# Second block: each weight product in two halves of query rows, with attention steps set between the halves

## The reference

```python
proj = xn @ w_in[l]
sb_q, sb_k, sb_v, sw_q, sw_k, sw_v, sb_z, sw_z, g_sb, g_sw = jnp.split(proj, offsets, axis=-1)
o_sb = stick_breaking_attention(...)          # 8 heads of 64
q = rope(sw_q...); k = rope(sw_k...)
o_sw = sliding_window_sink_attention(...)     # 16 query heads, 2 key heads, window 128
y_sb = (o_sb * silu(sb_z)) @ w_branch_sb[l]
y_sw = (o_sw * silu(sw_z)) @ w_branch_swa[l]
merged = sigmoid(g_sb) * y_sb + sigmoid(g_sw) * y_sw
h = h + merged @ w_out[l]
return rms_norm_2(h, final_norm_gain)
```

## Time and profile before

| | |
|---|---|
| median of 3 runs | 1552.54 us (1546.03, 1552.54, 1552.65) |
| the profiled execution, its own time | 1551.99 us |
| its span, first to last instruction | 1550.2 us |
| mean granted TensorE clock over the span | 0.983 of 2.4 GHz |
| TensorE busy | 1504.0 us |
| VectorE busy | 1116.3 us |
| ScalarE busy | 904.5 us |

### The profile page before, as it was taken

The page is one execution under the profiler, slowest core; times in us unless marked ns, Lnnn a source line. Parts: engine busy times, 40 slices in busy tenths (PEclk is TensorE's granted clock), DMA queues, the critical chain, the costliest instruction groups (busy, mean ns, idle before and its releaser), DMA issues.

```text
span 1550.2 us, 19263 instructions
## 1 busy us (share of the span) xinstructions
PE 1504.0 (97%) x7580; PEld 1263.5 (82%) x7580; DVE 1116.3 (72%) x975; ACT 904.5 (58%) x770; POOL 134.9 (9%) x118
## 2 busy tenths in 40 slices
PE   6999999999989999999999999999999999999998
PEld 6869998897768888888888888888877687777786
DVE  6985455389778888888888988979789743343455
ACT  5564433355646777776777767676766553343443
POOL 3600000062010000000000000000172100000000
PEclk9999999999989999999999999999999998998999
DMA  9358964463379999999999999999999442322241
GB/s 329 133 176 282 327 233 166 136 197 115 126 274 354 353 394 363 378 378 355 396 355 371 392 347 406 348 375 380 368 407 336 151 164 82 109 84 80 82 163 55
DMA packets 118810, 407.67 MB, mean 263 GB/s; under 512 B 5824, under 2 KB 31600, under 8 KB 118752
## 3 DMA queue, kind: packets, MB, share of 16 engines
q1 hardware_dynamic: 114576, 392.84, 69.2%
q0 software_dynamic: 3104, 10.22, 1.8%
q10 hardware_dynamic: 1072, 3.80, 0.6%
HBM read 400.02 MB, written 18.87 MB: 270 GB/s over the span
## 4 chain that ended last, share of the span: by engine, by line
PE 83%; DVE 11%; issue 2%; ACT 2%; DMA 2%; ACTq 0%; DVEq 0%; SPq 0%
PE ps L465 22%; PE ps L466 22%; PE ps L467 22%; DVE low L449 3%; DVE yT L1909 3%; PE ps L2586 1%; DVE low L455 1%; PE ps L2259 1%; DMA raw<-in_moe_wg 1%; ACT high L444 1%; PE ps L1235 1%; DMA raw<-in_moe_wu 1%; PE ps L1256 1%; DVE xn L1846 1%; PE ps L1222 1%
## 5 line engine op out<-in xcount | busy, mean ns | idle before, releaser
L455 DVE TENSOR_TENSOR low<-raw,high 128x2816 fp32r<-128x2816 f32 (+1 forms) x168 | 522.1, 3124 | 99.7 <-ACT high L444 99.4
L444 ACT ACTIVATE high<-raw 128x2816 fp32r<-128x2816 f32 (+1 forms) x168 | 428.5, 2561 | 109.8 <-PE ps L467 53.6
L465 PE MATMUL ps<-high,xTm_hi 128*128 128x384 f32 (+2 forms) x1144 | 424.3, 371 | 13.3 <-DVE low L449 7.2
L466 PE MATMUL ps<-low,xTm_hi 128*128 128x384 f32 (+2 forms) x1144 | 419.1, 366 | 0.0
L467 PE MATMUL ps<-high,xTm_lo 128*128 128x384 f32 (+2 forms) x1144 | 419.0, 366 | 0.0
L449 DVE TENSOR_TENSOR low<-raw,high 128x2816 fp32r<-128x2816 f32 (+2 forms) x72 | 202.9, 2827 | 76.2 <-ACT high L438 75.9
L465 PEld LDWEIGHTS ps<-high,xTm_hi 128*128 128x128 f32 x1144 | 215.6, 188 | 48.7 <-DVE low L449 7.9
L467 PEld LDWEIGHTS ps<-high,xTm_lo 128*128 128x128 f32 x1144 | 215.7, 189 | 28.1
L466 PEld LDWEIGHTS ps<-low,xTm_hi 128*128 128x128 f32 x1144 | 215.6, 188 | 27.8
L438 ACT ACTIVATE high<-raw 128x2816 fp32r<-128x2816 f32 (+2 forms) x72 | 168.4, 2344 | 117.6 <-PE ps L467 99.5
L465 PE MATMUL ps<-high,eT_hi 128*128 128x512 f32 x352 | 142.7, 405 | 0.9 <-DVE low L455 0.8
(11 more groups left out here) (406 smaller groups left out, 1818.9 us busy)
## 6 DMA issues: line engine op xcount, KB each, us to landing
raw<-in_moe_wg SPq DMA_DIRECT2D x64, 1408.0 KB, 8.1
raw<-in_moe_wu SPq DMA_DIRECT2D x64, 1408.0 KB, 9.0
raw<-in_moe_wd SPq DMA_DIRECT2D x48, 1536.0 KB, 8.5
rawb<-in_w_in SPq DMA_DIRECT2D x25, 1024.0 KB, 5.1
raw<-in_w_in SPq DMA_DIRECT2D x16, 1024.0 KB, 7.3
raw<-in_moe_wd SPq DMA_DIRECT2D x16, 1024.0 KB, 8.6
raw<-in_ffn_wg SPq DMA_DIRECT2D x8, 1408.0 KB, 9.8
raw<-in_ffn_wu SPq DMA_DIRECT2D x8, 1408.0 KB, 8.1
```

The costliest lines, as they stand in the source:

```text
L444: nc.scalar.activation(high[:, j % SPLITS, 0:n], raw[:, j % RAWS, 0:n], ACT.Copy).then_inc(hi_made, 1)
L455: nc.vector.tensor_tensor(low[:, j % SPLITS, 0:n], raw[:, j % RAWS, 0:n], f(high[:, j % SPLITS, 0:n]), ALU.subtract).then_inc(lo_made, 1)
L465: nc.tensor.matmul(out, xh, wh, start=first, stop=False)
L466: nc.tensor.matmul(out, xh, wl, start=False, stop=False)
```

## The change

`fill(c)` is taken apart: `half_fill(c, 0)` does the 12 matmuls of b = 0, with the wait for the split weights, `half_fill(c, 1)` those of b = 1, with the release of the slot. `fill(c)` is still both in a row. The waits and the semaphores are the same. Then 14 of the sets from 8 to 23 (8, 9, 11, 13, 14, 15 and 16 to 23) are multiplied in halves with steps of attention between, and some steps change their place against the products: `sb_output(0)` and `sb_output(3)`, `sb_scores(2)` and `sb_scores(3)`, `query_transposes(3)`, `sw_scores(1)`, and in the head loop `sw_output(h)` for h below 6, which goes between the halves, or `pt_fill(h, 1)` for the last two, which goes between them.

```diff
         def fill(c):
 
+            half_fill(c, 0)
+            half_fill(c, 1)
+
+        def half_fill(c, b):
+
             n = tile_of(c)
             first, last = c == TILE_CHUNKS[n][0], c == TILE_CHUNKS[n][-1]
-            pe.wait_ge(blo_made, c + 1)
-            for b in range(NB):
-                if first:
-                    pe.wait_ge(tile_read, 2 * (n - 1) + b + 1)
-                    if n == Q0 and b == 0:
-                        pe.wait_ge(mv_read, 2)
-                mm = block(c, b)
-                if last and b == 0:
-                    mm.then_inc(half_filled, 1)
-            mm.then_inc(bw_used, 1)
+            if b == 0:
+                pe.wait_ge(blo_made, c + 1)
+            if first:
+                pe.wait_ge(tile_read, 2 * (n - 1) + b + 1)
+                if n == Q0 and b == 0:
+                    pe.wait_ge(mv_read, 2)
+            mm = block(c, b)
+            if b:
+                mm.then_inc(bw_used, 1)
+            elif last:
+                mm.then_inc(half_filled, 1)
@@
         sb_suffix(0)
-        fill(8)
+        half_fill(8, 0)
         sb_output(0)
+        half_fill(8, 1)
         sb_suffix(1)
+        half_fill(9, 0)
         sb_scores(2)
-        fill(9)
+        half_fill(9, 1)
         sb_output(1)
         fill(10)
         sb_suffix(2)
+        half_fill(11, 0)
         sb_scores(3)
-        fill(11)
+        half_fill(11, 1)
         sb_output(2)
         fill(12)
         sb_suffix(3)
+        half_fill(13, 0)
         key_transposes()
         query_transposes(0)
-        fill(13)
         sb_output(3)
+        half_fill(13, 1)
         query_transposes(1)
         query_transposes(2)
+        half_fill(14, 0)
         query_transposes(3)
-        fill(14)
+        half_fill(14, 1)
         sw_scores(0)
-        fill(15)
+        half_fill(15, 0)
         sw_scores(1)
+        half_fill(15, 1)
         for h in range(8):
             pt_fill(h, 0)
             if h + 2 < 8:
                 sw_scores(h + 2)
-            pt_fill(h, 1)
+                pt_fill(h, 1)
+                half_fill(16 + h, 0)
+            else:
+                half_fill(16 + h, 0)
+                pt_fill(h, 1)
             if h == 7:
                 sw_transposes(0)
-            fill(16 + h)
-            sw_output(h)
+                half_fill(16 + h, 1)
+                sw_output(h)
+            elif h == 6:
+                half_fill(16 + h, 1)
+                sw_output(h)
+            else:
+                sw_output(h)
+                half_fill(16 + h, 1)
```

## The result

| | before | with the change |
|---|---|---|
| median of 19 runs of each | 1552.3 us (1545.41 to 1561.82) | 1543.92 us (1534.83 to 1549.85) |
| ratio, 95% interval | | 0.9943 (0.9926 to 0.9961) |
| profiled execution, own time and span | 1551.99, 1550.2 us | 1539.97, 1538.1 us |
| mean granted clock over that span | 0.983 | 0.989 |

The forecast was 1544.3 us. The change is faster by 0.57%, with an interval that reaches from 0.39 to 0.74%.

The account below looks back on a forecast made before the run. TensorE, 97% busy, was taken as bound by its granted clock and its waits: 1551.99 - 8.0 - 1.7 + 0.9 + 1.1 = 1544.3 us. The range was 1537.5 to 1552.5 us.

Parts of the forecast that it names:

- What bounds: Second block, 1290 to 1442 us: six busy half-clock stretches, 37.0 us together, lose 17.2 us; TensorE's waits only 1.7.
- The rival in which the order does not move the clock: Clock falls as often and as long whatever stands behind a narrow run; 1552.3 us; chance 0.11.
- (a): Behind the eight long 64-column runs: product or half follows, six falls of 3.3 us, 19.8 us low, 8.0 us gained.
- Price of a microsecond at the low clock: In weight products, a wide matmul takes 0.23 us at full clock, 0.43 at low; each low microsecond loses 0.465 us.
- (b): Head steps 6 and 7 and query_transposes(3): half products cover waits of 0.7, 0.7 and 0.3 us; 1.7 us gained.
- (c): Head loop, h = 1, 3, 5: pt_fill(h, 1) waits 0.3 us for ScalarE's copy behind the split; 0.9 us lost.
- (d): Eleven new product entries behind narrow steps open slower, 0.1 us each; 1.1 us lost, possibly nothing or 2 us.
- (e): Earlier sb_output(0) and sb_scores(2), later loads: cost nothing; 1 to 2 us if the rotations' cover were gone.
- The first rival: Two or fewer falls remain, as narrow runs have wide work on both sides; 14.1 us gained, 1538.2 us; chance 0.14.
- The third: Head loop: pt_fill(h, 1) and sw_output wait for copies of pt, 4.8 us over six steps, 1549.1 us; chance 0.08.
- The fourth: Half product too short to bring the clock back, next narrow steps run low; four falls give 1562 us; chance 0.06.

Follow-up runs that it names:

- e2_rest: The changed kernel with every output step back in its old place, sb_output(3) behind the whole of 13; 1551.03 us, 0.9999 of before.
- e5_copy_first: The changed kernel with ScalarE's copy of pt ahead of the next weight set's split in the head loop; 1543.21 us, 0.9944 of before.

## Why the prediction was right, point by point

- **What bounds.** Right. The 17.3 us less at the low clock are 7.1 of 8.2 us. The rival in which the order does not move the clock falls: the output steps' places alone took 12.7 us from the low time, with TensorE busy in every low stretch. The rule of the Trainium skill that stood beside it ("TensorE: Matmul & The Clock Gate", section "Why this matters for your kernels": avoid idle gaps between bursts) is not enough here: the trace shows falls without a gap (6.60 of 6.60 us busy at 0.50).
- **(a), 17.2 us less low clock, 8.0 us.** The size was right (17.3 and 7.1), the picture half right. In the head loop each fall lasts as long as a fall under a product, fourteen times out of fourteen. But I kept the number of falls at six and each at 3.3 us: the profiled execution had three, and one of them, behind sb_output(2), lasted 6.8 us with a whole product behind it. The same happened behind sb_output(1) in e2_rest and behind sb_output(0) in e5_copy_first. Of the ten falls behind an sb_output with a product or half of one next, these three lasted 6.8 us and seven 3.4 us. The three began 0.7 to 0.8 us ahead of the output step's end, the others, and all fourteen of the head loop, at most 0.6 us ahead of it or behind it. No experiment set that distance, so it is a pattern and not a shown cause. In the change the clock is low from 1333.70 us and the product starts at 1334.44:

```profile
1333.70:1334.40 0.70, 0.70 (x4) 0.51 (x3) 0.24 (x1) 0.47 (x1) 0.00 (x0) 0.50 0.00 0
```

```profile
1334.44 0.80 PE L465 MATMUL ps<-highb,xTm_hi 128*128 128x512 f32 x1
```

  Over many executions the sizes agree all the same. The kernels without a fall in this part keep 16 to 20 us of low time elsewhere in the program. By estimate, then, some 16 of the change's 34.1 us lie in this part, and some 33 of before's 51.4; I had 19.8 and 37.0. Both were about 4 us too high, and the errors cancel in the difference, which is luck. The profiled execution of before, with 52.7 us by its clock of 0.983, was a usual one.
- **Price of a microsecond at the low clock.** 0.465 from the pace of the matmuls; 0.41 over all executions, 0.48 over the change's own. The pace was a fair guide. Part of the low time lies elsewhere in the program, where TensorE also waits; whether that is why 0.41 is the smaller is not shown.
- **(b), 1.7 us of waits gone.** Right, all three.
- **(c), a new wait of 0.9 us.** Right to the tenth: 0.9 us, three times, 0.3 at most, and removed by the order of ScalarE's list. What I did not price is what (b) hides: with (c) alone the wait at h = 6 grows to 2.1 us, and half the change is worth little (1549.45).
- **(d), 0.1 us for each new entry.** Right where the timeline shows it (2.89 us a half); the sum of 1.1 us is below what the runs can tell. By the rest, the change is 1.1 us below before, by the slope of 0.48 it would be 0.1 above; my sum of (b) to (d) was 0.3 above.
- **(e), no cost.** Right for the changed kernel, as no other wait appeared. It was close: with the output steps alone sb_scores(2) waited 1.1 us for sb_read(0), behind the rotations, because no half product stood ahead of it.
- **The first rival, falls nearly vanish.** Right to leave it at a small chance for this change: its low time of 34.1 us is still 14 to 18 us above that of the kernels without a fall. It takes cut runs, and then it is worth 6 us and more on top. In single executions it did come about: the low time of the 19 reaches from 15.3 to 49.5 us, and four of them, with 24.6 us or less, have by the estimate above room for two falls at most.
- **The third, waits take the gain.** It did not come: 0.9 us of waits, and none for VectorE's copy of `pt`.
- **The fourth, slower.** A half product was enough in all fourteen falls of the head loop. It was not enough once: behind sb_output(0) in e5_copy_first the low clock ran through the whole half (1294.27 to 1299.55 us) and 0.85 us into the suffix step. The clock came back there, so the cost did not spread as the rival had it.

```profile
1299.55 1.01 PE L1159 MATMUL ps<-sb_x,csec 128*128 128x256 f32 x2
1300.40 0.39 PE L1160 MATMUL ps<-sb_x,csec 128*128 128x128 f32 x2
```

- **The number.** 1544.3 against 1543.92 us is closer than either side allows: the median of 19 executions that spread over 15 us is itself uncertain by about 1 us, and the start of my sum was one execution.

## What to carry to other kernels

Read the granted clock by stretches even where TensorE is 97% busy: its low stretches are invisible in the busy share, and in the profiled execution here they cost 17 us where the waits cost 1.7. What helped most was to break up the long runs of small matmuls with wide ones (low time 51.4 to 20.0 us); where they stayed whole, wide work behind them helped in the head loop, and not always elsewhere. When a step is moved ahead of the release of a buffer, ask what the engine that waits for the release does before the next thing that you need from it. And time such a kernel over many executions, with the clock of each beside its span.

## What the runs showed of the hardware

- The clock falls under busy work. Six stretches before, with TensorE busy in all of each, start at the end of runs of 3.24 or 2.8 us of matmuls of 64 columns, from 0.3 us ahead of it to 1.5 us behind it. With the runs cut in half and wide matmuls between, there is not one in three kernels' profiles.
- Wide work does not always end a fall at once: of the 24 falls with a product or half of one next, three lasted 6.8 us and 21 lasted 3.4 us. The three had matmuls of 512 columns from 0.8 us after their start on, and one of them outlasted the half product.
- The same program varies by 16 us (1545.41 to 1561.82) over 19 executions, and its low time from 37 to 75 us over 52; the kernels without falls in this part vary by 3 to 6 us over six.
- More work inside the loop can be quicker: the cut kernels add entries of 0.1 us each and gain 13 to 17 us.
